# Expert layers of a two-block network on one core: the experts' weights built in one pass, and 16 instead of 24 dense tokens served from gathered rows

## The reference, cut to what matters

```python
def peer_ffn(h, w_q, sub_keys, u_tab, v_tab):
    ...
        q = (xc @ w_q).reshape(t, PEER_HEADS, 2, PEER_QDIM // 2)
        sc = jnp.einsum('thpc,hpnc->thpn', q, sub_keys).astype(jnp.float32)
        v_half, i_half = lax.top_k(sc, PEER_TOPK_HALF)
        ...
        top_s, pos = lax.top_k(cand, PEER_TOPK)
        expert = jnp.take_along_axis(cand_idx, pos, axis=-1)
        g = jax.nn.softmax(top_s, axis=-1)
        u = u_tab[expert]
        act = jax.nn.gelu(jnp.einsum('thkd,td->thk', u, xc).astype(jnp.float32), approximate=False)
        w = (g * act).astype(xc.dtype)
        return jnp.einsum('thk,thkd->td', w, v_tab[expert])
```

## Time and profile before

| what | us |
|---|---|
| median of 3 executions | 1953.17 |
| lowest, highest | 1952.59, 1963.65 |
| span of the profiled execution, first to last instruction | 1954.7 |
| busy: PE, DVE, ACT, POOL | 1914.8, 1647.7, 835.5, 514.5 |

### The profile page before, as it was taken

The page is one execution under the profiler, slowest core; times in us unless marked ns, Lnnn a source line. Parts: engine busy times, 40 slices in busy tenths (PEclk is TensorE's granted clock), DMA queues, the critical chain, the costliest instruction groups (busy, mean ns, idle before and its releaser), DMA issues.

```text
span 1954.7 us, 34888 instructions
## 1 busy us (share of the span) xinstructions
PE 1914.8 (98%) x12514; PEld 1713.6 (88%) x12514; DVE 1647.7 (84%) x3368; ACT 835.5 (43%) x1410; POOL 514.5 (26%) x452
## 2 busy tenths in 40 slices
PE   8999999999999999999999999999999999999998
PEld 7888887878999999988888787899999998888886
DVE  6899886886899479699999977779975996999998
ACT  6557644555210100165555566551111003555565
POOL 0000000001346633242325300023465332421461
PEclk9999999999999999999999999999999999999999
DMA  6544334526799999888789964268999997887996
GB/s 257 226 172 188 125 109 135 181 68 201 232 402 387 404 409 369 310 275 279 260 313 393 355 190 130 87 191 343 403 393 405 407 350 251 286 278 270 359 406 240
DMA packets 142248, 539.22 MB, mean 276 GB/s; under 512 B 17820, under 2 KB 17948, under 8 KB 139456
## 3 DMA queue, kind: packets, MB, share of 16 engines
...
...
## 4 chain that ended last, share of the span: by engine, by line
PE 75%; DVE 8%; DMA 2%; ACT 2%; issue 2%; ACTq 0%; SPq 0%; DVEq 0%
PE bank L2605 30%; PE bank L350 10%; PE bank L352 10%; PE bank L351 10%; PE bank L2638 5%; PE bank L2639 5%; PE bank L2476 3%; DMA wbuf<-in_peer_v 2%; DVE x_tok L2433 1%; DVE tile_lo L280 1%; DVE tile_lo L3014 1%; PE bank L2561 1%; ACT tile_hi L272 0%; DVE w_parts L3018 0%; PE bank L1594 0%
## 5 line engine op out<-in xcount | busy, mean ns | idle before, releaser
L2605 PE MATMUL bank<-h_dense,wbuf 128*128 128x168 f32 x4096 | 602.0, 307 | 3.8 <-issue 3.5
L2605 PEld LDWEIGHTS bank<-h_dense,wbuf 128*128 128x128 f32 x4096 | 585.1, 190 | 5.1 <-issue 4.4
L2754 ACT ACTIVATE tile_hi<-wbuf 128x1024 fp32r<-128x1024 f32 x248 | 263.2, 1062 | 253.3 <-DMA wbuf<-in_peer_v 162.0
L2409 POOL DMA_INDIRECT e_gbuf<-in_peer_v,e_row_at x128 | 245.4, 1917 | 418.3 <-DVE x_tok L2433 381.2
L3014 DVE TENSOR_TENSOR tile_lo<-wbuf,tile_hi 128x1024 fp32r<-128x1024 f32 x256 | 308.1, 1217 | 18.6 <-ACT tile_hi L2716 13.3
L2727 ACT ACTIVATE e_hidden<-bank 128x336 f32<-128x336 f32 x128 | 57.8, 451 | 538.3 <-PE bank L2605 487.7
L2638 PE MATMUL bank<-tile_hi,w_parts 128*128 128x512 f32 x512 | 205.1, 401 | 1.7 <-DVE w_parts L3018 1.5
L2409 POOL DMA_INDIRECT e_gbuf<-in_peer_rows,e_row_at x128 | 143.9, 1124 | 238.1 <-DVE e_dots L2427 151.7
L2386 POOL DMA_DIRECT2D e_stage<-e_stage x48 | 23.8, 512 | 670.1 <-DVE e_stage L2806 670.1
L2639 PE MATMUL bank<-tile_lo,w_parts 128*128 128x512 f32 x512 | 199.7, 390 | 0.0
L351 PE MATMUL bank<-tile_lo,w_parts 128*128 128x512 f32 x512 | 199.4, 389 | 0.0
...
## 6 DMA issues: line engine op xcount, KB each, us to landing
wbuf<-in_peer_u SPq DMA_DIRECT2D x128, 1024.0 KB
wbuf<-in_peer_v SPq DMA_DIRECT2D x256, 512.0 KB
...
```

The costliest lines, as they stand in the source:

```text
L2409: nc.gpsimd.indirect_dma_start(out=gbuf[:, b, :], out_offset=None, in_=table[:, :], in_offset=bass.IndirectOffsetOnAxis(rows, axis=0)).the ...
L2605: last = nc.tensor.matmul(bank[:, j // 2 % 2, j % 2 * S + EXTRA:j % 2 * S + DENSE], deep[:, slot, k * P:(k + 1) * P], h_dense[:, k, PLAIN] ...
L2754: nc.scalar.activation(tile_hi[:, slot, 0:D], ring[:, slot, 0:D], ACT.Copy).then_inc(hi_done, 1)
```

## The change

The few are 16 tokens instead of 24, so 176 are plain. The weights of all 128 first keys are made in one pass, in 22 groups of 8 plain tokens and 4 groups of 4 few tokens, all inside stage 1: behind tiles 53, 55, 58, 60, 63, 65 and so on to 115 (`WEIGHTS_AT`). The transposes of the picks stand behind tile 50; the few's shares times activations are turned later, by one transpose behind tile 81. A group of 8 fills banks 2 and 3 together. VectorE makes both one-hots with one instruction and the high share part with another; ScalarE makes the low part (few: the third part) with one small instruction for each token (`rest_hots`). ScalarE writes a group's weights for keys still ahead into `hidden` (`keep_weights`); VectorE multiplies those for keys already evicted (`weigh`). From pair 27 on, ScalarE evicts the groups already weighted to `raw_acts`, and VectorE multiplies them into `hidden` (`multiply`). The one-hots lie in the memory of `tile_lo`, free in stage 1. Stage 2 has no weights any more. The diff, cut to its core:

```diff
-BLOCKS = ((0, 16), (16, 8))
+BLOCKS = ((0, 16),)
...
-    PARTS = ((0, 80, 6), (80, 48, 8))
-    FIRST_KEYS = PARTS[0][1]
     WEIGHT_ONE = 4096.0
...
+    GROUP, FEW_GROUP = 8, 4
+    PLAIN_GROUPS, FEW_GROUPS = (DENSE - EXTRA) // GROUP, EXTRA // FEW_GROUP
+    NGROUPS = PLAIN_GROUPS + FEW_GROUPS
+    KEYS_TURNED = 50
+    WEIGHTS_AT = [53 + 5 * n // 2 for n in range(NGROUPS)]
+    PAIR_OF = [tile // 2 for tile in WEIGHTS_AT]
+    FEW_TURNED_BEHIND, FEW_TURNED = 11, WEIGHTS_AT[11] + 1
...
+    raw_acts = [sb(f"{tag}_raw_acts{b}", [P, 2, DENSE - EXTRA]) for b in range(2)]
...
+    def tokens_of(n):
+
+        return EXTRA + GROUP * n if n < PLAIN_GROUPS else FEW_GROUP * (n - PLAIN_GROUPS)
+
+    def keys_hot(n):
+
+        size, dt = (GROUP, F16) if n < PLAIN_GROUPS else (FEW_GROUP, B16)
+        return hot_keys[n % 2][:, 0:2 * size * NKEYS].bitcast(dt).rearrange("p (r a m) -> p r a m", a=NKEYS, m=2)
+
+    def shares_hot(n):
+
+        size, dt, parts = (GROUP, F16, 2) if n < PLAIN_GROUPS else (FEW_GROUP, B16, 3)
+        return hot_shares[n % 2][:, 0:parts * size * NKEYS].bitcast(dt).rearrange("p (w i a m) -> p w i a m", w=parts, a=NKEYS, m=2)
+
+    def one_hots(dve, n):
+
+        plain = n < PLAIN_GROUPS
+        size, at, pairs = (GROUP, n, GROUP // 2) if plain else (FEW_GROUP, n - PLAIN_GROUPS, FEW_GROUP // 2)
+        if n >= 2:
+            dve.wait_ge(weights_done, n - 1)
+        if n == PLAIN_GROUPS:
+            dve.wait_ge(picks_kept, FEW_KEPT)
+        rows = (plain_T if plain else few_keys_T)[:, at, :].rearrange("p (r m) -> p r m", m=2)
+        nc.vector.tensor_tensor(keys_hot(n), wide[:, :, :].unsqueeze(1).to_broadcast([P, 2 * pairs, NKEYS, 2]),
+                                rows.unsqueeze(2).to_broadcast([P, 2 * pairs, NKEYS, 2]), ALU.is_equal).then_inc(hots_done, 1)
+        dve.wait_ge(hots_done, 2 * n + 1)
+        tokens = slice(size * at, size * at + size)
+        shares = [share_hi[:, EXTRA:DENSE]] if plain else [few_T[:, part, :] for part in range(2)]
+        for part, row in enumerate(shares):
+            by_pairs = row[:, tokens].rearrange("p (i m) -> p i m", m=2).unsqueeze(2).to_broadcast([P, pairs, NKEYS, 2])
+            made = nc.vector.tensor_tensor(shares_hot(n)[:, part, :, :, :], keys_hot(n)[:, 0:pairs, :, :], by_pairs, ALU.mult)
         made.then_inc(hots_done, 1)
...
+    def rest_hots(act, n):
+
+        plain = n < PLAIN_GROUPS
+        size, row, part, first = (GROUP, share_lo, 1, tokens_of(n)) if plain else (FEW_GROUP, few_third, 2, tokens_of(n))
+        act.wait_ge(hots_done, 2 * n + 1)
+        if n >= 2:
+            act.wait_ge(weights_done, n - 1)
         for m in range(size):
+            made = nc.scalar.activation(shares_hot(n)[:, part, m // 2, :, m % 2], keys_hot(n)[:, m // 2, :, m % 2], ACT.Copy,
+                                        scale=row[:, first + m:first + m + 1])
+        made.then_inc(rest_hots_done, 1)
...
+    def weights(pe, n):
+
+        plain = n < PLAIN_GROUPS
+        size, parts = (GROUP, 2) if plain else (FEW_GROUP, 3)
+        second, shares = keys_hot(n)[:, size // 2:size, :, :], shares_hot(n)
+        pe.wait_ge(hots_done, 2 * n + 2)
+        pe.wait_ge(rest_hots_done, n + 1)
+        if n:
+            pe.wait_ge(weighed, min(n, PLAIN_GROUPS))
+            pe.wait_ge(weights_kept, n if plain else max(PLAIN_GROUPS, n - 1))
+        if n == FEW_TURNED_BEHIND + 1:
+            pe.wait_ge(picks_kept, FEW_KEPT)
+        for m in range(size):
+            first = 2 + (m // 4 if plain else n % 2)
             for part in range(parts):
-                last = nc.tensor.matmul(bank[:, 2 + b, m * keys:(m + 1) * keys], second[:, m // 2, :, m % 2],
-                                        weighted_first[:, part, m // 2, :, m % 2],
-                                        start=(part == 0), stop=(part == parts - 1))
+                last = nc.tensor.matmul(bank[:, first, m % 4 * NKEYS:(m % 4 + 1) * NKEYS], second[:, m // 2, :, m % 2],
+                                        shares[:, part, m // 2, :, m % 2], start=(part == 0), stop=(part == parts - 1))
         last.then_inc(weights_done, 1)
...
+    def behind(n):
+
+        return 2 * PAIR_OF[n] + 2
+
+    def weigh(dve, n):
+
+        dve.wait_ge(weights_kept, n + 1)
+        keys_made, first = slice(0, behind(n)), tokens_of(n)
+        part = hidden[:, keys_made, first:first + GROUP]
+        nc.vector.scalar_tensor_tensor(out=part, in0=made_weights(n)[:, keys_made, :], scalar=1.0 / WEIGHT_ONE, in1=part,
+                                       op0=ALU.mult, op1=ALU.mult).then_inc(weighed, 1)
...
+    def keep_weights(act, n):
+
+        act.wait_ge(weights_done, n + 1)
+        first = tokens_of(n)
+        if n < PLAIN_GROUPS:
+            ahead = slice(behind(n), NKEYS)
+            nc.scalar.activation(hidden[:, ahead, first:first + GROUP], made_weights(n)[:, ahead, :], ACT.Copy,
+                                 scale=1.0 / WEIGHT_ONE).then_inc(weights_kept, 1)
         else:
-            nc.vector.scalar_tensor_tensor(out=part, in0=made, scalar=1.0 / WEIGHT_ONE, in1=part, op0=ALU.mult, op1=ALU.mult).then_inc(weighted, 1)
...
+    def groups_before(f):
+
+        return sum(pair < f for pair in PAIR_OF[0:PLAIN_GROUPS])
+
+    MULTIPLIED = [f for f in range(NKEYS // 2) if groups_before(f)]
+
+    def multiply(dve, f):
+
+        groups = groups_before(f)
+        stop = EXTRA + GROUP * groups
+        dve.wait_ge(bank_free, 2 + f + 1)
+        dve.wait_ge(weights_kept, groups)
+        part = hidden[:, 2 * f:2 * f + 2, EXTRA:stop]
+        nc.vector.tensor_tensor(part, raw_acts[f % 2][:, :, 0:GROUP * groups], part, ALU.mult).then_inc(multiplied, 1)
+
+    def taken_at(tile):
+
+        return min(38 + (tile - 48) * (DOTS - 38) // (121 - 48), DOTS + max(0, tile - 121) // 2)
+
+    TAKEN, LAST_TAKE = (34, 38, 40), 123
+    EXPS_AT, FEW_AT = (11, 23), 35
+    ACTS_AT, ACTS = 58, (slice(0, 48), slice(48, SHARED))
+    FEW_MULTIPLIED, FEW_KEPT = 8, 13
...
-        with pe.Fori(0, FIRST_WEIGHING - 1) as r:
+        with pe.Fori(0, KEYS_TURNED // STEP) as r:
             for j in range(STEP):
                 experts(r, STEP, 0, j)
...
+        for tile in range(KEYS_TURNED // STEP * STEP, NKEYS):
+            experts(0, STEP, tile // STEP * STEP, tile % STEP)
+            if tile == KEYS_TURNED:
+                pe.wait_ge(soft_step, 4 * NT)
...
                 for row in range(3):
-                    dense_turned(bank[:, 2 + row // 2, row % 2 * S:row % 2 * S + DENSE], lambda t: pick[:, t, row, :]).then_inc(picks_turned, 1)
-        with pe.Fori(0, FIRST_LOOPS) as q:
-            for j in range(FIRST_LOOP):
-                experts(q, FIRST_LOOP, FIRST_KEYS, j)
-                if j in FIRST_AT:
-                    weights(pe, 0, len(FIRST_AT) * q + FIRST_AT[j], FIRST_AT[j] % 2, False, PARTS[0][2])
-        for j in range(NKEYS - FIRST_END):
-            experts(0, STEP, FIRST_END, j)
-            if j in END_AT:
-                weights_of(pe, 0, END_AT[j])
+                    dense_turned(bank[:, 2 + row // 2, row % 2 * S:row % 2 * S + DENSE], lambda t: pick[:, t, row, :]).then_inc(columns_turned, 1)
+            if tile in WEIGHTS_AT:
+                weights(pe, WEIGHTS_AT.index(tile))
+            if tile == FEW_TURNED:
+                pe.wait_ge(soft_step, 4 * NT + 1)
+                pe.wait_ge(weighed, FEW_TURNED_BEHIND + 1)
+                pe.wait_ge(weights_kept, FEW_TURNED_BEHIND + 1)
+                nc.tensor.transpose(bank[:, 2, FEW], acts_few[FEW, :], ident[FEW, FEW]).then_inc(columns_turned, 1)
 
...
-        with pe.Fori(0, SECOND_LOOPS) as q:
-            for j in range(SECOND_LOOP):
-                values(q, SECOND_LOOP, 0, j)
-                if j in SECOND_AT:
-                    weights(pe, 1, len(SECOND_AT) * q + SECOND_AT[j], SECOND_AT[j] % 2, False, PARTS[1][2])
...
-        with pe.Fori(0, ROUNDS - 1 - WEIGHING) as r:
+        with pe.Fori(0, ROUNDS - 1) as r:
             for j in range(STEP):
-                values(r, STEP, WEIGHING * STEP, j)
+                values(r, STEP, 0, j)
...
             act.wait_ge(used, M_U + 2 * f + 2)
-            nc.scalar.activation(hidden[:, 2 * f:2 * f + 2, PLAIN], bank[:, f % 2, :].rearrange("p (a t) -> p a t", t=S)[:, :, PLAIN],
-                                 ACT.Gelu).then_inc(bank_free, 1)
+            made = bank[:, f % 2, :].rearrange("p (a t) -> p a t", t=S)
+            groups = groups_before(f)
+            if groups:
+                if f in MULTIPLIED[2:]:
+                    act.wait_ge(multiplied, MULTIPLIED.index(f) - 1)
+                last = nc.scalar.activation(raw_acts[f % 2][:, :, 0:GROUP * groups], made[:, :, EXTRA:EXTRA + GROUP * groups], ACT.Gelu)
+            if groups < PLAIN_GROUPS:
+                later = slice(EXTRA + GROUP * groups, DENSE)
+                last = nc.scalar.activation(hidden[:, 2 * f:2 * f + 2, later], made[:, :, later], ACT.Gelu)
+            last.then_inc(bank_free, 1)
...
```

(113 more changed lines are left out.)

132 lines of the change are left out of this document (43 added, 89 removed).

## The result

The kernel after takes 1991.12 us (median of 4 runs, 1989.57 to 1994.16), the kernel before beside it 1957.49 us (4 runs): a ratio of 1.018, 95% interval 1.016 to 1.020, so 34 us slower. The forecast was 1978 us, between 1963 and 1991. The direction was right; the size was 13 us short, and the time lies 0.1 us above the range.

What follows compares the result with a forecast made beforehand. TensorE was taken as the bound, with VectorE and DMA nearly full. Terms 27.3 - 14.2 + 4.7 + 10 - 3 = +24.8 us on the median of 1953.2 gave 1978 us, range 1963 to 1991.

Steps and rivals of the forecast that it cites:

- Columns, +27.3: Stage 1: products 176 instead of 168 columns wide cost 6.7 ns more for each of 4096 instructions, +27.3 us.
- Weights, -14.2: TensorE's weight products: 31.2 us a layer removed, 24.1 us a layer added, so -14.2 us for both layers.
- third rival: Small products cost 70 to 80 ns, or start at tile 50 and first groups late: +8 to +20 us; chance 0.14.
- The chain through ScalarE, +10: Stage 1: after five even-tile groups a layer, TensorE stands 1.0 us for ScalarE's eviction, `keep_weights` and `rest_hots`: +10 us.
- the chain closes in time: Rival: `rest_hots` pieces cost 0.20 us or less, so stage 1's five stands shrink or vanish; about 1968 us; chance 0.27.
- The wait behind tile 81, +4.7: Stage 1: TensorE idles 2.25 us a layer before the few's transpose, +4.5 us, and 0.2 for transposes.
- Stage 1 in sum, 340: Stage 1 of a layer should take 313.0 + 13.7 + 24.1 - 17.7 + 7.3 = 340 us.
- the unexplained stands of before: Stage 1: 1.8 us of unexplained "issue" waits, 3.5 for both layers, were taken to stay.
- Stage 2, -3: Stage 2: TensorE's loss of 3 us in the first layer and 0.5 in the second should go, -3 us.
- the second rival: VectorE or DMA, not TensorE, sets stage 2's pace, so less VectorE work shortens it; over 1% faster: chance 0.03.
- The anchor: Forecast's base: profiled execution 1954.7 us, 1.5 us above the median of three, 1953.2 us.
- The late start: Stage 1: start at tile 50 and first groups late in both layers; costed at nothing, up to 3 us a layer.

Runs made afterwards that it cites:

- e0: Not a follow-up run: the first of the kernel's two layers in a trace; its stage 1 takes 313.0 us in before, 340.4 in after.
- before again: The kernel before, unchanged, profiled a second time as a second program: 1956.0 us, ratio 1.0003 to before.
- thin gathers: Against the kernel after with every group behind an odd tile: gathers of value rows fetch 16 of their 128 rows; 1962.0 us, ratio 1.003 to before.

## Why the prediction was right or wrong

- **Columns, +27.3:** right. In the first 50 tiles of e1 an instruction of 176 columns steps by 149.3 ns in after, one of 168 columns by 142.6 in before again: 27.3 us over 4096. The width alone measured 13.4 us a layer.
- **Weights, -14.2:** right. A group of 16 takes 666.97 - 666.05 = 0.92 us and 0.04 before it, one of 12 about 0.7; 24.0 us a layer. One product steps by (1.08 - 0.218) / 15 = 57 ns, so the third rival's dearer products did not come. The Trainium skill (TensorE: Matmul & The Clock Gate, Back-to-back issue gap) gives about 81 ns for a weight load and product of 128 columns in a stream; here the trace decides against that figure.
- **The chain through ScalarE, +10:** right in place and number, a little small: 10.1 us shown, 12 with the edges. The pieces of `rest_hots` start every 0.293 us, just above my upper bound of 0.29, and with the tail of the last the eight take 2.48 us against 2.1 assumed. I had fitted a cheaper piece from rows of other shapes. The estimate of 0.29 us by the figures of the Trainium skill (ScalarE: Activation LUTs, What ACT_TABLE_LOAD costs), which I had set aside, agrees with the trace. The rival "the chain closes in time" fell with it.
- **The wait behind tile 81, +4.7:** right, 3.8 us for the two waits, and 1.7 more for the lower clock behind the first. That a wait costs more than its length was no term of mine.
- **Stage 1 in sum, 340:** measured 340.4 and 338.9, but two of its parts were off against each other: the unexplained stands of before, "which stay", belonged to that one execution (2.4 us a layer), and the edges of the waits and the clock took their place. That the sum came out was luck.
- **Stage 2, -3, "the loss should go":** this step failed. I put the loss on VectorE, since it was nearly full, and let the gain of VectorE's time stand for the transfers, which I had named beside it as nearly full. Two signs came as forecast, VectorE at 87% and a DMA share of 0.92, below 0.95, and yet TensorE lost 4.7 and 3.9 us where 0.8 us were to be left in both layers together. The thin gathers show the cause in its place: fewer bytes of gathered rows beside the value tiles take the loss away, with the same work on VectorE. About the same number of gathers (54 in place of 52) in a stage 12 us shorter raised the DMA share from 0.87 to 0.92, and value tiles landed in 6.2 us (median) in after, against 5.0 in before again. In before the loss stands in the last 56 tiles, at a DMA share of 0.95; but there VectorE is busy 126.7 of 131 us too, and no run takes the two apart in that kernel. By the sum both stages 2 should have taken 611.4 - 27.0 - 3 = 581.4 us, and they took 589.2: 7.8 of the 8.0 us by which the span of after exceeds the 1979.5 forecast. Stage 1 was 1.1 us below its sum, and 1.3 us came from outside. That VectorE's time would give back more (the second rival) did not happen either: a product steps by 0.227 us in before again, in after and with thin gathers.
- **The anchor:** 5 us more lie between span and median, most of them in the median of before. Three runs gave 1953.2 us for before; in the four comparisons made since it is 1955.5 to 1957.5.
- **The late start** of the third rival was not met in after, where VectorE was ready 4.0 us before TensorE asked. The kernel with one pass and 168 columns used that up and more.
